# Token-major projections in half-contraction chunks, in a two-block transformer kernel

## What is computed

```
def fox_mixer(q, k, v, f_logit, b_f):                      # layer B
    log_f = jax.nn.log_sigmoid(f_logit + b_f)              # 12 forget gates for each token
    log_f_cum = jnp.cumsum(log_f, axis=1)
    out = causal_block_attention(qh, kh, vh, FOX_DIM ** -0.5, log_f_cum)
...
            proj = hn @ w_in_b[j]
            q, k, v, f_logit, q_m, gate = split_cols(
                proj, [MAIN_WIDTH, MAIN_WIDTH, MAIN_WIDTH, FOX_HEADS, MEM_WIDTH, MIX_WIDTH])
...
    ia = (h @ w_in)[..., 1024:1536]                        # values of the recurrent layer
    v  = (h @ w_in)[..., 1024:2048]                        # values of the mLSTM layer
```

## Time and profile before

| | us |
|---|---|
| median of 3 timed runs | 1937.67 (1937.56 to 1942.08) |
| span of the profiled execution | 1938.3 |
| PE busy / DVE / ACT / POOL | 1886.2 / 1106.1 / 762.3 / 789.9 |
| gate0 to the start of layer B's attention | 323.1 to 500.4 |

### The profile page before, as it was taken

The page is one execution under the profiler, slowest core; times in us unless marked ns, Lnnn a source line. Parts: engine busy times, 40 slices in busy tenths (PEclk is TensorE's granted clock), DMA queues, the critical chain, the costliest instruction groups (busy, mean ns, idle before and its releaser), DMA issues.

```text
span 1938.3 us, 24077 instructions
## 1 busy us (share of the span) xinstructions
PE 1886.2 (97%) x9993; PEld 1501.0 (77%) x9993; DVE 1106.1 (57%) x1567; ACT 762.3 (39%) x1181; POOL 789.9 (41%) x361
## 2 busy tenths in 40 slices
PE   7999999999999999999999999999989999999998
PEld 5878566978667698977788888877967878888886
DVE  5324767657776669535688647855911455512543
ACT  5436654421564431265433222324465333312332
POOL 2224743434663462123344344343433434444442
PEclk9999999999999999999999999999999999999999
DMA  8224104555204352122253534452430222233221
GB/s 259 68 58 121 37 17 126 158 175 178 80 23 131 98 164 66 44 87 77 88 162 120 166 128 160 133 169 88 150 112 23 87 87 87 87 104 113 79 70 69
DMA packets 212061, 205.97 MB, mean 106 GB/s; under 512 B 21352, under 2 KB 209004, under 8 KB 211953
## 3 DMA queue, kind: packets, MB, share of 16 engines
q1 hardware_dynamic: 209369, 200.36, 32.6%
q0 software_dynamic: 1472, 3.72, 0.7%
q10 hardware_dynamic: 1111, 0.36, 0.1%
HBM read 201.44 MB, written 2.11 MB: 105 GB/s over the span
## 4 chain that ended last, share of the span: by engine, by line
PE 88%; DVE 4%; ACT 3%; POOL 2%; issue 1%; DMA 1%; ACTq 0%; SPq 0%; DVEq 0%
PE bank L550 56%; PE bank L1161 17%; PE bank L799 2%; PE bank L823 2%; PE bank L972 1%; PE bank L851 1%; PE bank L490 1%; POOL wl L2457 1%; DMA ring<-in_w_mem_kv 1%; PE bank L1234 1%; ACT probs L1532 1%; POOL probs L2491 1%; PE bank L573 1%; PE bank L1223 1%; DVE acc L1876 1%
## 5 line engine op out<-in xcount | busy, mean ns | idle before, releaser
L2457 POOL TENSOR_TENSOR wl<-ring,wh 128x2048 fp32r<-128x2048 f32 (+4 forms) x145 | 614.8, 4240 | 876.4 <-ACT wh L1377 874.0
L1377 ACT ACTIVATE wh<-ring 128x2048 fp32r<-128x2048 f32 (+5 forms) x147 | 254.7, 1733 | 318.6 <-PE bank L550 126.1
L550 PE MATMUL bank<-xfh,wh 128*128 128x512 f32 x704 | 275.5, 391 | 0.2
L550 PE MATMUL bank<-xfl,wh 128*128 128x512 f32 x704 | 274.1, 389 | 0.0
L550 PE MATMUL bank<-xfh,wl 128*128 128x512 f32 x704 | 274.0, 389 | 0.0
L1876 DVE SCALAR_TENSOR_TENSOR acc<-ring,cs,acc 128x256 f32<-128x256 f32 x336 | 226.5, 674 | 12.0
L550 PEld LDWEIGHTS bank<-xfh,wh 128*128 128x128 f32 x704 | 132.1, 188 | 31.7 <-DVE xfl L1946 2.6
L550 PEld LDWEIGHTS bank<-xfh,wl 128*128 128x128 f32 x704 | 132.2, 188 | 27.7
L550 PEld LDWEIGHTS bank<-xfl,wh 128*128 128x128 f32 x704 | 132.2, 188 | 26.9
L2318 DVE SCALAR_TENSOR_TENSOR x<-bank,mod,x 128x512 f32<-128x512 f32 x48 | 34.7, 750 | 180.5 <-PE bank L1161 180.5
L1161 PE MATMUL bank<-hsph,wh 128*128 128x512 f32 x352 | 137.5, 391 | 0.0
(11 more groups left out here) (417 smaller groups left out, 4100.7 us busy)
## 6 DMA issues: line engine op xcount, KB each, us to landing
ring<-in_ada_w SPq DMA_DIRECT2D x48, 1024.0 KB, 5.2
ring<-in_ffn_w_in SPq DMA_DIRECT2D x44, 1024.0 KB, 5.1
ring<-in_w_in_b SPq DMA_DIRECT2D x14, 1024.0 KB, 5.3
ring<-in_even_w_in SPq DMA_DIRECT2D x14, 1024.0 KB, 5.1
ring<-in_ffn_w_out SPq DMA_DIRECT2D x16, 768.0 KB, 4.5
ring<-in_odd_w_in SPq DMA_DIRECT2D x12, 1024.0 KB, 5.3
ring<-in_ffn_w_out SPq DMA_DIRECT2D x16, 640.0 KB, 4.2
ring<-in_w_out SPq DMA_DIRECT2D x8, 1024.0 KB, 4.9
```

Of the source, the lines that this page charges most:

```text
L550: mm = eng.matmul(o, l_, r_, start=(first and i == 0), stop=(last and i == 2))
L1377: eng.activation(wh[:, m % SPLIT, h:w], ring[:, n % RING, h:w], ACT.Copy).then_inc(wh_ready, 1)
L2457: eng.tensor_tensor(wl[:, m % SPLIT, h:w], ring[:, n % RING, h:w], wh[:, m % SPLIT, h:w].bitcast(F32), ALU.subtract).then_inc(wl_ready, 1)
```

## The change

Three projections with the tokens as stationary operand are cut differently: layer B's values, the values `ia` of the recurrent layer, and the values of the mLSTM layer. A chunk is now four contraction tiles by up to 512 columns, and PE keeps four banks (one for each block of 128 tokens) open over two such chunks. In layer B the twelve forget columns are projected with the values (two groups of 390 columns); the separate f chunk is gone, ACT puts the twelve columns into `fcol`, and PE turns them to rows after qm. The chunks of layer B are now gate0, v0a, v0b, v1a, v1b, qm, gate1 and so on: the same number of chunks, and the list of where the `ada` chunks stand is the same 13, but it now starts behind the second chunk of the layer (v0a), not the third. DVE's order of `ada` steps has four before qm in both.

```diff
+    def halves(name, w, lo, cols):
+        v = w.rearrange("(t p) n -> p t n", p=P)
+        return [(name, v[:, t:t + KT // 2, lo:lo + cols], KT // 2, cols) for t in (0, KT // 2)]
...
-    add(gates[:1] + k8("in_b.f", w, 3 * MAIN, 3 * MAIN + P))
-    add(k8("in_b.v", w, 2 * MAIN, 3 * MAIN) + k8("in_b.qm", w, 2316, 2572) + gates[1:] + k8("in_b.q", w, 0, MAIN)
+    add(gates[:1])
+    add(halves("in_b.v", w, 2 * MAIN, VF) + halves("in_b.v", w, 2 * MAIN + VF, VF)
+        + k8("in_b.qm", w, 2316, 2572) + gates[1:] + k8("in_b.q", w, 0, MAIN)
         + k8("in_b.k", w, MAIN, 2 * MAIN), 13 * (1,))
...
+            def token_group(stage, g, owner, ready, xs, lag):
+                bs = []
+                for half in range(2):
+                    m, ws = chunk(stage)
+                    kts, cols = ws[0].shape[1], ws[0].shape[2]
+                    for blk in range(NB):
...
+                        for k in range(kts):
+                            for i, (a_, b_) in enumerate(((0, 0), (0, 1), (1, 0))):
+                                mm = eng.matmul(bs[blk][:, 0:cols], xs[b_][:, half * kts + k, blk * P:(blk + 1) * P],
+                                                ws[a_][:, k, :], start=(half == 0 and k == 0 and i == 0),
+                                                stop=(half == 1 and k == kts - 1 and i == 2))
...
-            m, ws = chunk("in_b.f")
-            features(("f",), "dve", ws, slice(0, P), xb, KT, "x_b")
-            chunk_done(m)
...
-            project("in_b.v", 3, "act", "x_b", xb, tok=True, lag=1)
+            for g in range(2):
+                token_group("in_b.v", g, "act", "x_b", xb, 1)
             project("in_b.qm", 1, "dve", "x_b", xb, lag=1)
+            wait_emptied(pe, ("in_b.v", 1, NB - 1))
+            b = bank(("f",), "dve")
+            for blk in range(NB):
+                t = eng.transpose(b[0:HEADS, blk * P:(blk + 1) * P], fcol[:, blk, :], ident)
+            done(t)
...
-            project("even.ia", 2, "act", "x_even", xe, tok=True, lag=1)
+            token_group("even.ia", 0, "act", "x_even", xe, 1)
...
-            project("odd.v", 3, "act", "x_odd", xo, tok=True, lag=1)
+            token_group("odd.v", 0, "act", "x_odd", xo, 1)
...
-            project("odd.v", 1, "act", "x_odd", xo, tok=True, lag=1, t=3)
+            token_group("odd.v", 1, "act", "x_odd", xo, 1)
...
+            for b in range(NB):
+                split_weights(tile_chunk[index[("in_b.v", 1, b)]] + 2)
+                v = take(act, ("in_b.v", 1, b), "act")
+                eng.activation(fcol[:, b, :], v[:, MAIN - VF:VF], ACT.Copy, scale=token_rs[:, b:b + 1])
...
+            split_weights(tile_chunk[index[("in_b.qm", 0)]] + 2)
+            split_weights(tile_chunk[index[("in_b.gate", 2)]] + 2)
             wait_emptied(act, ("f",))
...
-            empty_scaled(("f",), frow[0:HEADS, 0, :], slice(0, HEADS))
-            ada_steps(1)
+            ada_steps(4)
...
-            ada_steps(3)
             for t in range(2):
                 empty_scaled(("in_b.qm", t), qm[:, t, :])
+            empty(("f",), fr[0], (slice(0, HEADS), slice(0, S)))
+            chain.link(eng.memset(fr[5], 1.0))
             for t in range(2, KT):
                 if t % 2 == 0:
                     ada_steps(1)
                 empty_scaled(("in_b.gate", t), gate[:, t, :])
+                if t == 3:
+                    log_sigmoid(fr[0], fr[1], fr[2], f_log)
```

More of the change, by code:

```diff
@@ L34 @@
 FT = FFN // P
+VF = (MAIN + HEADS) // 2
 FFN_PARTS = [(0, 12), (12, 22)]
@@ L160, in weight_plan @@
                           ("vb", 3072, ()), ("ga", 1536, (1, 1))):
-        add(k8("even." + name, w, lo, lo + 512), behind)
+        add(halves("even." + name, w, lo, 512) if name == "ia" else k8("even." + name, w, lo, lo + 512), behind)
     add(k8("even_out", a["even_w_out_2"][0], 0, D), (0, 1))
@@ L178, in weight_plan @@
     w = a["odd_w_in_2"][0]
-    add(k8("odd.qk", w, 0, 256) + k8("odd.gates", w, 3008, 3088) + k8("odd.qk", w, 256, 1024) + k8("odd.v", w, 1024, 2048)
+    add(k8("odd.qk", w, 0, 256) + k8("odd.gates", w, 3008, 3088) + k8("odd.qk", w, 256, 1024)
+        + halves("odd.v", w, 1024, 512) + halves("odd.v", w, 1536, 512)
         + k8("odd.og", w, 2048, 3072), 5 * (0,) + 3 * (1,))
@@ L343, in two_block_kernel @@
         frow = at("frow", 24, 6, S)
+        fcol = var[:, 0, P // 2:P // 2 + NB * HEADS].rearrange("p (b h) -> p b h", h=HEADS)
         hq, hk, pf, va = (at(n, 8 * i, 4, S) for i, n in enumerate(("hq", "hk", "pf", "va")))
@@ L648, in project @@
                         ada_sums(lag)
+            def token_group(stage, g, owner, ready, xs, lag):
[4 more added lines that the diff above has]
+                    for blk in range(NB):
+                        if half == 0:
+                            bs.append(bank((stage, g, blk), owner))
+                            pe.wait_ge(xl_ready, SPLIT_AT[ready] + kts)
+                        else:
+                            pe.wait_ge(xl_ready, SPLIT_AT[ready] + 2 * kts)
+                            tile_chunk[blk - NB] = m
+                        for k in range(kts):
[3 more added lines that the diff above has]
+                                                stop=(half == 1 and k == kts - 1 and i == 2))
+                        if half == 1:
+                            done(mm)
+                    if half == 0:
+                        mm.then_inc(w_part, 1)
+                        counts["part"] += 1
+                        chunk_done(m, counts["part"])
+                    else:
+                        chunk_done(m)
+                    ada_sums(lag)
             pe.wait_ge(loaded_c, 16)
@@ L952, in _ @@
             mark["att1"] = len(released)
-            for s in range(3):
-                wait_emptied(pe, ("in_b.v", s, NB - 1))
             pe.wait_ge(frows_moved, 16 * 2 * HEADS)
@@ L1272, in _ @@
             pe.wait_ge(qk_silu, KT)
-            wait_emptied(pe, ("odd.v", 3, NB - 1))
+            wait_emptied(pe, ("odd.v", 1, NB - 1))
             ml_weights(0)
@@ L1594, in _ @@
             act.wait_ge(loaded_p, 48)
-            split_weights(tile_chunk[index[("f",)]] + 3)
+            half_bank = (slice(0, P), slice(0, CHUNK))
+            wait_emptied(act, ("token_rs",))
+            for b in range(NB):
+                empty(("in_b.v", 0, b), v1[:, b, 0:VF], part=(slice(0, P), slice(0, VF)), scale=token_rs[:, b:b + 1])
+            for b in range(NB):
+                split_weights(tile_chunk[index[("in_b.v", 1, b)]] + 2)
+                v = take(act, ("in_b.v", 1, b), "act")
+                eng.activation(fcol[:, b, :], v[:, MAIN - VF:VF], ACT.Copy, scale=token_rs[:, b:b + 1])
+                eng.activation(v1[:, b, VF:MAIN], v[:, 0:MAIN - VF], ACT.Copy, scale=token_rs[:, b:b + 1]
+                               ).then_inc(emptied["act"], 1)
+            split_weights(tile_chunk[index[("in_b.qm", 0)]] + 2)
+            split_weights(tile_chunk[index[("in_b.gate", 2)]] + 2)
             wait_emptied(act, ("f",))
@@ L1600, in _ @@
             log_of(frow[0:HEADS, 0, :], frow[0:HEADS, 1, :], f_log)
[L1601 to L1606, removed]
             for t in range(2, KT):
                 silu(t)
+                if t < 4:
+                    continue
                 act.wait_ge(frows_set, 32)
                 act.wait_ge(frows_ready, 1)
-                for h in (2 * t - 4, 2 * t - 3):
+                for h in range(3 * t - 12, 3 * t - 9):
                     eng.dma_start(qf[HD:HD + 1, h, :], frow[h:h + 1, 3, :]).then_inc(frows_moved, 16)
@@ L1642, in _ @@
                 eng.activation(hk[:, t, :], b[:, :], ACT.Sigmoid, scale=-1.0).then_inc(emptied["act"], 1)
-            for s in range(2):
-                for b in range(NB):
-                    empty(("even.ia", s, b), va[:, b, CHUNK * s:CHUNK * (s + 1)], part=half_bank)
+            for b in range(NB):
+                empty(("even.ia", 0, b), va[:, b, :])
             for t in range(4):
@@ L1790, in decays @@
                     eng.activation(dec[h % 2][:], dec[h % 2][:], ACT.Exp, scale=-1.0).then_inc(dec_exp, 1)
-            for s in range(4):
+            for s in range(2):
                 for b in range(NB):
-                    empty(("odd.v", s, b), vo[:, b, CHUNK * s:CHUNK * (s + 1)], part=half_bank)
-                    if (s, b) == (3, 0):
+                    empty(("odd.v", s, b), vo[:, b, S * s:S * (s + 1)])
+                    if (s, b) == (1, 1):
                         wait_emptied(act, ("gcol",))
@@ L2163, in _ @@
                 empty_scaled(("in_b.gate", t), gate[:, t, :])
+                if t == 3:
+                    log_sigmoid(fr[0], fr[1], fr[2], f_log)
+                    chain.link(eng.tensor_tensor_scan(fr[3], fr[5], fr[2], 0.0, ALU.mult, ALU.add))
+                    eng.tensor_scalar(fr[4], fr[3], -1.0, None, ALU.mult).then_inc(frows_ready, 1)
             for name, dst, scale in (("in_b.q", qf, HD ** -0.5), ("in_b.k", kf, 1.0)):
```

15 lines of the change are left out of this document (5 added, 10 removed).

## The result

The changed kernel takes 1980.87 us (median of 4 runs, 1979.47 to 1987.96) against 1938.44 for the kernel before beside it: ratio 1.0219, 95% interval 1.0201 to 1.0237. That is 2.2% slower, 4.9 us above the forecast of 1976 and inside its range. The profiled span is 1980.2 us (1938.3 before). Of all executions behind this document one took 3796.32 us (the kernel with v0a's split later): its ratio leaves that one out, and its trace is not used.

The account below looks back on a forecast made before the run. PE's columns plus its waits bound the kernel (88% of the span PE's own work). 1938.3 + 40.2 (layer B) - 1.3 (`ia`) - 0.4 (mLSTM) = 1976.8, forecast 1976 us, 2.0% slower; own range 1971 to 1981, wider range 1962 to 1986.

Parts of the forecast that it names:

- The lost lead: Layer B: loads wait for an `ada` step one later, behind tiles that wait for PE; attention starts 40.2 us later.
- A7 ends: DVE's `ada` step behind qm's tiles, for which gate2's load now waits instead of A6; takes 4.0 us, ending 398.9.
- Rival 1: Layer B: the lead doesn't matter, a ring turn takes at most PE's 10.9 us; 1933 us; chance 0.10, halved at the bound.
- Rival 3: Layer B: dearer values or landings, 390 columns cost as 512, or loads crowd; 1983 to 1985 us; chance 0.10.
- The turn: Layer B, q1 to k2: POOL's low part, the `ada` step held until it ends, load, split, POOL; 16.0 us each.
- the slow clock: PE in layer B: 1.2 GHz after gaps adds 2.2 us per chunk; from q1 to k2 it costs only in the last.
- rival 2: Layer B: shorter turns, DVE isn't stopped, gaps too short for the slow clock; 1968 us; chance 0.15.
- 5.7 us of columns: PE in layer B: 288 matmuls of 256 and 24 of 512 become 192 of 390 and four transposes; saves 5.7 us.
- the start of layer B: Root uncovered without f, v0a's longer split 0.5 us late; values from 343.5 instead of 346.8, 3.3 of f's 5.4 us kept.
- `ia`: Recurrent layer's values: 192 matmuls of 256 columns become 96 of 512, saving 1.3 us that count, since PE alone is the chain.
- The mLSTM's saving: Its values projection ends 2.7 us earlier, but hidden by a longer wait behind it; 0.4 us counted, bounds 0 and 2.7.

Follow-up runs that it names:

- the changed kernel's second trace: The changed kernel, nothing altered, run again beside the one with a later forget-gate scan: 1983.26 us, ratio 1.0222 to the kernel before.
- the kernel with q1's split too: The one with three edits, plus ACT splitting q1 ahead of the last twelve row transfers: 1939.03 us, ratio 0.9991 to the kernel before.
- the one with three edits: Changed kernel with `ada` chunks again starting behind v0b, v0a split behind the residual loop, q0 split ahead of row transfers: 1938.51 us, ratio 0.9999 to before.

## Why the prediction was right

**The lost lead** (the largest term, 40.2 us) is shown three times over. By the steps, forecast and measured:

| step | forecast | after |
|---|---|---|
| values start | 343.5 | 345.25 |
| qm's low part ends | 380.9 | 382.66 |
| A7 ends | 398.9 | 401.82 |
| gate2's low part ends | 411.0 | 413.74 |
| gate3's | 429.9 | 432.62 |
| q0's | 445.9 | 447.99 |
| q1's | 461.9 | 464.18 |
| k1's | 510 | 511.76 |
| attention starts | 540.6 | 543.19 |

Every step is late by 1.8 to 2.9 us. Of that 1.75 stand at the first step, and 0.47 of these lie ahead of layer B, where this execution was later already. A7 is 1.2 us later still: the forecast gave qm 10.9 us at full clock, and PE took 12.1 (382.72 to 394.87), with the clock at 0.61 from 383 to 386. Rival 1 (the lead doesn't matter) fell with the turns of 15.8 to 16.2 us. Rival 3 fell too: 390-column matmuls start 0.17 to 0.19 us apart, near the interpolated 0.176.

**The turn: the length is right, partly by luck.** Landing (5.4 to 5.9) and split came as forecast. But the forecast let POOL hold back every `ada` step until it ends. In the five turns that bring q1 to k2 that stop cost 0.7, 2.2, 0.0, 1.9 and 0.7 us. In the turn shown above DVE waited 9.78 us for PE's gate3, until 445.81, and POOL only stretched the first operation of the step (1.05 us for 0.35). The chain that ended last runs through every second chunk (gate3, q1, k0, k2), and through PE's matmuls in it; some of its pieces, in order of time:

```profile
464.23 12.75 PE bank L558 x45
...
479.85 0.38 DVE acc L1917
...
483.88 5.37 DMA ring<-in_w_in_b
...
489.34 1.93 ACT wh L1414
...
491.33 4.51 POOL wl L2499
...
495.88 12.13 PE bank L558 x45
```

From 464.23 to 495.88 that is 31.65 us for two turns. The forecast had this way only among its bounds, as 29.7 us with 10.9 us of PE. It said that the slow clock costs nothing more but in the last turn; here it made these chunks of PE longer, and so the way over two chunks came out at the same 16 us. The stretches of two turns after, with busy time of PE, PEld, DVE, ACT and POOL, the granted clock and DMA:

```profile
446.00:462.00 16.00, 12.03 (x66) 9.23 (x65) 8.79 (x16) 4.67 (x5) 4.32 (x2) 1.00 0.44 133
462.00:478.00 16.00, 13.77 (x64) 10.83 (x64) 6.83 (x11) 1.92 (x1) 4.67 (x2) 0.79 0.42 132
```

Ahead of q1, in the second, PE had waited 4.97 us; ahead of q0, in the first, 1.24. Of rival 2 (DVE isn't stopped, and the gaps are too short for the slow clock) the first half thus held in some turns, and the second didn't. The two ways lie close: in the changed kernel's second trace the chain runs over q0, q2 and k1, where POOL's stop is 2.4 and 1.9 us. An estimate for the whole of layer B: attention came 42.4 us later from the common start, the waits make 34.3 of it, and the new cut saves 5.7 us of columns by the forecast; so some 14 us are work at the lower clock.

**Mis-sized: the start of layer B.** The forecast had ACT's longer split (0.5 us) as the price of v0a ahead of the norm. It left out POOL's longer low part behind it. The timelines of POOL and DVE there, before and then after:

```profile
318.56 2.35 POOL L2457 TENSOR_TENSOR wl<-ring,wh 128x1024 fp32r<-128x1024 f32 x1 [4.53 <-ACT wh L1377]
...
320.52 0.93 DVE L2122 TENSOR_TENSOR x<-x,o 128x512 f32<-128x512 f32 x1
```

```profile
319.47 3.48 POOL L2499 TENSOR_TENSOR wl<-ring,wh 128x1560 fp32r<-128x1560 f32 x1 [4.98 <-ACT wh L1414]
...
321.43 2.07 DVE L2165 TENSOR_TENSOR x<-x,o 128x512 f32<-128x512 f32 x1
```

DVE's residual add takes 2.07 us for 0.93, and ends 0.55 us behind POOL. The experiment that moved this split won 1.8 us at that place. In the earlier trace rows I had seen DVE stop under POOL, and had counted it only where I looked.

**Mis-sized: `ia`.** Forecast 1.3 us, measured 0.7: from its first matmul to that of the next stage it is 23.36 us (731.00 to 754.36), and 24.02 before (688.22 to 712.24). Its second half waits, in the chain in order of time:

```profile
725.28 4.96 DVE acc L1919
730.23 0.02 issue
730.25 5.94 DMA ring<-in_even_w_in
736.19 0.02 issue
736.21 1.93 ACT wh L1414
738.13 0.07 issue
738.21 4.63 POOL wl L2499
742.84 0.04 issue
742.88 11.19 PE bank L673 x48
```

It is layer B's turn again in small: one operation of an `ada` step (0.5 us as a rule) is stopped for 4.96, and load, split and low part follow, PE waiting 0.48 us. With `ia` and odd.v cut alone, where no such wait shows, it takes 22.81 us, 1.2 less than before: there the forecast's size is nearly right.

**The mLSTM's saving** was hidden, as forecast: 0.6 us came through (forecast 0.4). But the projection itself became only 1.7 us shorter and not 2.7, and a wait of 0.65 us for its last chunk is most of the difference; so the wait behind it grew from 7.00 to 8.02 us and not to 9.

**What remains of the 4.9 us:** the spans differ from the forecast by 3.4 us (1980.2 for 1976.8): 2.6 at attention and 0.6 in `ia`, less 0.2 that the mLSTM gave more than forecast. What is left is within the scatter between executions: the changed kernel's second trace has attention at 540.83, and its timed runs lie between 1979.47 and 1987.96.

## What to carry to other kernels

Where a ring of slots serves two consumers, the order of the loads and the order of each consumer's own work are one schedule: shifting the list by one place made a chunk wait for a step that stands behind the very tiles that the late chunk feeds. Count, for each load, which step frees its slot and what stands ahead of that step, before counting what a recut saves. A saved wait is worth nothing until the next one behind it on the same engine has been read: here q0's moved to q1, and the scan's to A9.

## What the runs showed of the hardware

**An earlier attention can end later.** Of thirteen traces, two show the granted clock at half for a stretch behind attention's start, 17.1 and 13.7 us long: the kernel with q1's split too, and the changed kernel's second trace. Windows of the first of these two, with busy time of PE, PEld, DVE, ACT and POOL, then the granted clock:

```profile
495.00:500.00 5.00, 3.51 (x14) 1.60 (x13) 3.90 (x12) 2.60 (x11) 1.85 (x3) 1.00 0.94 310
...
505.00:510.00 5.00, 5.00 (x18) 3.34 (x17) 2.26 (x7) 2.96 (x11) 1.13 (x3) 0.50 0.00 0
510.00:515.00 5.00, 5.00 (x13) 2.36 (x13) 2.44 (x8) 1.81 (x7) 3.42 (x4) 0.50 0.00 0
```

0.50 is 1.2 GHz. What PE did before: it waited for the first probabilities, 1.6 us here and 4.0 us in the changed kernel's second trace, and 0.8 to 1.5 us in the eleven others, whose clock stayed at 1.00 there. That the longer wait let the clock fall is compatible with these rows, but not shown: no experiment isolates it, and 1.58 us in the one and 1.54 in one of the others hardly differ. The 4.0 us come from ACT: in its timeline of that trace, a split that waits for its load stands ahead of the first exponential (in the changed kernel's first trace the split was done in time, at 541.77):

```profile
543.24 1.91 ACT L1414 ACTIVATE wh<-ring 128x2048 fp32r<-128x2048 f32 x1 [16.10 <-DMA ring<-in_w_out]
545.05 0.35 ACT L1569 ACTIVATE probs<-bank,nmx 128x128 f32<-128x128 f32 x1
```

From attention's start to the end these two took 1443.6 and 1443.8 us, the others 1435.1 to 1438.4. So, counted from the common start, the kernel with q1 reached attention 1.5 us ahead of the one with three edits, and ended 6.2 us behind it (1641.9 and 1635.7). Its fastest timed run, 1933.58, has a mean clock of 0.995, and its runs at 0.989 and 0.990 took 1939.0 to 1942.7. Gains of 2 to 3 us disappear in this.

**DVE stops under POOL, and not only in the ring's turns.** The residual add above ended 0.55 us behind POOL's low part, and the operation at 725.28 ended 0.30 behind POOL's (725.30 and 4.64 us long). The Trainium skill (SBUF — State Buffer, section "SBUF: two separate sides") says that a VectorE operation with two inputs in SBUF and a GpSimd operation that reads SBUF share a port pair: whichever starts first holds it for its whole instruction, and the other fully blocks. The trace agrees on the block: 2.07 us for an add of two SBUF tiles that takes 0.68 where POOL is idle. Which one was first can't be told at 725.28 against 725.30. Not every DVE operation stops: q1's tiles, read from a PSUM bank, take 2.81 us for four at 477.00, under POOL's low part (475.50 to 480.05), as k2's last two take 1.39 with POOL idle.
